# A hybrid transformer block on one core: the masked key products of two scan chunks as one block-diagonal 128 by 128 weight tile

## What is computed

```python
def rwkv_scan(S0, r, w, k, v, a, b, reverse):
    def step(S, inp):
        r_t, w_t, k_t, v_t, a_t, b_t = inp
        sa = jnp.einsum('bhij,bhj->bhi', S, a_t)
        S = S * w_t[:, :, None, :] + sa[..., :, None] * b_t[:, :, None, :] + v_t[..., :, None] * k_t[:, :, None, :]
        return S, jnp.einsum('bhij,bhj->bhi', S, r_t)
    ...
    S, ys = lax.scan(step, S0, xs, reverse=reverse)
```

## Time and profile before

| | |
|---|---|
| median of 3 runs | 2294.09 us (2288.39 to 2295.02) |
| the profiled execution | 2289.43 us, its span 2287.4 us |
| granted TensorE clock, mean over the span | 0.974 |
| PE busy | 2162.4 us, 95% |
| PE weight loads (PEld, beside PE) | 1780.5 us, 78% |
| DVE busy | 958.9 us, 42% |
| POOL busy | 872.0 us, 38% |
| ACT busy | 663.2 us, 29% |

### The profile page before, as it was taken

How to read it: one execution, slowest core, us unless ns; L and a number is a source line. 1 busy time by engine, 2 the same in 40 slices (tenths; PEclk the granted TensorE clock), 3 DMA queues, 4 the chain that set the end, 5 groups by cost and what they waited for, 6 DMA issues and landing times.

```text
span 2287.4 us, 44913 instructions
## 1 busy us (share of the span) xinstructions
PE 2162.4 (95%) x19484; PEld 1780.5 (78%) x19484; DVE 958.9 (42%) x1411; ACT 663.2 (29%) x1178; POOL 872.0 (38%) x602
## 2 busy tenths in 40 slices
PE   6999899989899999999999999989989989999997
PEld 3888477668778888888888778857759867888886
DVE  2002355386743723315142520335476645452452
ACT  3110366632412211102011320146652323221221
POOL 3333333172144224333242542235253144454454
PEclk9999999999997999999999899999999988999999
DMA  7311200210131112222123331120120042333231
GB/s 281 100 52 54 74 2 1 98 38 4 39 130 46 56 56 65 65 65 65 56 74 127 113 112 56 38 74 2 62 74 4 13 158 64 92 101 101 83 111 55
DMA packets 45463, 163.73 MB, mean 72 GB/s; under 512 B 5504, under 2 KB 5504, under 8 KB 45024
## 3 DMA queue, kind: packets, MB, share of 16 engines
q1 hardware_dynamic: 44480, 158.29, 21.2%
q0 software_dynamic: 800, 2.69, 0.4%
HBM read 158.86 MB, written 2.10 MB: 70 GB/s over the span
## 4 chain that ended last, share of the span: by engine, by line
PE 85%; DVE 6%; ACT 4%; issue 3%; POOL 1%; DMA 1%; SPq 0%; DVEq 0%; ACTq 0%; POOLq 0%
PE ps L1567 80%; PE ps L1893 3%; ACT flat L872 1%; DMA flat<-wmod_dram 1%; PE ps L2180 0%; DVE flat L1362 0%; DVE part_h L1436 0%; POOL flat L703 0%; DVE flat L1371 0%; DVE flat L1180 0%; DVE flat L1351 0%; POOL flat L614 0%; ACT hT L886 0%; POOL wparts L568 0%; DVE flat L1416 0%
## 5 line engine op out<-in xcount | busy, mean ns | idle before, releaser
L1567 PE MATMUL ps<-part_hi,wparts 128*128 128x512 f32 (+1 forms) x2640 | 701.9, 352 | 10.1 <-POOL wparts L568 5.9
L1567 PEld LDWEIGHTS ps<-part_hi,wparts 128*128 128x128 f32 x2640 | 468.0, 190 | 82.7 <-DVE part_h L1436 5.5
L1567 PE MATMUL ps<-part_h,wparts 128*128 128x512 f32 (+1 forms) x1320 | 462.9, 351 | 0.0
L1567 PE MATMUL ps<-flat 64*64 64x32 f32 (+8 forms) x8200 | 420.8, 257 | 29.9 <-DVE flat L1371 14.5
L1567 PEld LDWEIGHTS ps<-flat 64*64 64x64 f32 (+4 forms) x8200 | 322.0, 141 | 117.9 <-issue 92.1
L606 POOL TENSOR_TENSOR wparts<-flat,wparts 128x1024 fp32r<-128x1024 f32 x96 | 241.0, 2511 | 411.0 <-ACT wparts L1081 409.6
L1567 PE MATMUL ps<-part_mlp,wparts 128*128 128x512 f32 (+1 forms) x1152 | 309.9, 354 | 0.6 <-issue 0.6
L1567 PEld LDWEIGHTS ps<-part_h,wparts 128*128 128x128 f32 x1320 | 250.9, 190 | 33.8 <-issue 1.7
L1567 PEld LDWEIGHTS ps<-part_mlp,wparts 128*128 128x128 f32 x1152 | 204.9, 189 | 31.3 <-issue 0.7
L1567 PE MATMUL ps<-part_lo,wparts 128*128 128x512 f32 (+1 forms) x576 | 204.0, 354 | 0.0
L1558 DVE TENSOR_TENSOR flat<-flat,ps 128x768 f32<-128x768 f32 (+1 forms) x64 | 52.5, 820 | 355.7 <-PE ps L1567 355.7
(11 more groups left out here) (224 smaller groups left out, 2825.7 us busy)
## 6 DMA issues: line engine op xcount, KB each, us to landing
flat<-w_dram SPq DMA_DIRECT2D x128, 512.0 KB, 3.6
flat<-wmod_dram SPq DMA_DIRECT2D x88, 512.0 KB, 5.9
flat<-win_dram SPq DMA_DIRECT2D x40, 512.0 KB, 3.6
flat<-wout_dram SPq DMA_DIRECT2D x16, 512.0 KB, 3.6
hT<-wmod_dram SPq DMA_DIRECT2D x8, 512.0 KB, 7.7
xT<-xT_dram SPq DMA_DIRECT2D x8, 384.0 KB, 6.4
flat<-rope_dram SPq DMA_DIRECT2D x2, 1024.0 KB, 6.5
out_dram<-xT SPq DMA_DIRECT2D x8, 256.0 KB, 2.1
```

Of the source, the lines that this page charges most:

```text
L1567: return pe.matmul(out, lhsT, rhs, start=start, stop=stop)
```

## The change

The AB part of each half moves out of `ABR` into a new place `DIAG[x][g]`, where each pair of direction and head has a 128 by 128 tile: AB of chunk 0 in the upper left block, AB of chunk 1 in the lower right block, and zeros in the other two. The X group then has 8 matmuls over all 128 rows and columns, each with the same 32 moving columns on 128 partitions. On DVE one mask of 1024 columns becomes three instructions: one for AB of chunk 0 on 64 partitions, one for AB of chunk 1 on the other 64, and one for R on 128 partitions, each of 512 columns. Only the third adds to `s_abm[x]`. ACT writes the tiles with zeros once in a layer, in four copies of 512 columns, before its first evacuation of the recurrence, and DVE waits for that before the first half of step 0. R is packed closer, and its readers follow.

```diff
+        DIAG = ((HALF[0] + 512, F_WORK + W_SCAN + 2 * SCAN_HALF), (RING + 5 * 256, HALF[1] + 512))
...
                 act.wait_ge(s_rp, 12 * l + 12)
                 nc_.activation(gtok[:, 4:6, :], ps[:, 1024:1536].rearrange("p (b f) -> p b f", b=2), ACT.Copy).then_inc(s_rpe, 1)
+                act.wait_ge(s_modps, 5 * l + 4)
+                act.wait_ge(s_side, 7 * l + 4)
+                act.wait_ge(s_prep, 3 * l + 2)
+                for x, g in ((0, 0), (1, 0), (1, 1), (0, 1)):
+                    ins = nc_.activation(cells(-1, DIAG[x][g], [1, 512]), km[:, M_AB:M_AB + 1].to_broadcast([P, 512]), ACT.Copy)
+                ins.then_inc(s_gate, 1)
...
-                        V.tensor_tensor(cells(-1, h + ABR, [256, 4], [1, 256]), bank(-1, o, [256, 4], [1, 256]),
-                                        km[:, M_AB:M_AB + 256].unsqueeze(1).to_broadcast([P, 4, 256]),
+                        if s == 0:
+                            dve.wait_ge(s_gate, 3 * l + 2)
+                        for c in range(2):
+                            V.tensor_tensor(cells(c, DIAG[x][0] + 64 * c, [DIAG[x][1] - DIAG[x][0], 2], [P, 4], C1),
+                                            bank(c, o, [P, 2], [256, 4], C1),
+                                            bass.AP(km, 64 * c * NKM + M_AB, [[NKM, 64], [P, 2], [0, 4], C1]), ALU.mult)
+                        V.tensor_tensor(cells(-1, h + ABR, [P, 4], [64, 2], C1), bank(-1, o + 64, [256, 4], [P, 2], C1),
+                                        bass.AP(km, M_AB + 64, [[NKM, P], [0, 4], [P, 2], C1]),
                                         ALU.mult).then_inc(s_abm[x], 1)
...
                                 for p in range(2):
                                     for f in range(2):
-                                        for c in range(2):
-                                            ins = mm(bank(c, o + g * P + (2 * p + f) * 32, [1, 32]),
-                                                     cells(c, h + ABR + p * 512 + f * 256 + g * P, C1),
-                                                     cells(c, h + TN + g * (256 + half) + (2 * p + f) * 64,
-                                                           [2 * half, 32 // half], [1, half]))
+                                        ins = mm(bank(-1, o + g * P + (2 * p + f) * 32, [1, 32]),
+                                                 cells(-1, DIAG[x][g] + (2 * p + f) * P, [1, P]),
+                                                 cells(-1, h + TN + g * (256 + half) + (2 * p + f) * 64,
+                                                       [2 * half, 32 // half], [1, half]))
                             ins.then_inc(s_X[x], 1)
...
-                                    q, r = h + ABR + p * 512 + f * 256 + g * P + 64, h + TOKS + g * 256 + f * P + p * 64
+                                    q, r = h + ABR + p * 256 + f * P + g * 64, h + TOKS + g * 256 + f * P + p * 64
```

More of the change, by code:

```diff
@@ L1970, in _ @@
                     if n == 2:
-                        pe.wait_ge(s_gate, 2 * l + 1)
+                        pe.wait_ge(s_gate, 3 * l + 1)
                         pe.wait_ge(s_rtab, 64 * (l + 1))
@@ L2098, in _ @@
                                     for f in range(2):
-                                        for c in range(2):
-                                            ins = mm(bank(c, o + g * P + (2 * p + f) * 32, [1, 32]),
-                                                     cells(c, h + ABR + p * 512 + f * 256 + g * P, C1),
-                                                     cells(c, h + TN + g * (256 + half) + (2 * p + f) * 64,
-                                                           [2 * half, 32 // half], [1, half]))
+                                        ins = mm(bank(-1, o + g * P + (2 * p + f) * 32, [1, 32]),
+                                                 cells(-1, DIAG[x][g] + (2 * p + f) * P, [1, P]),
+                                                 cells(-1, h + TN + g * (256 + half) + (2 * p + f) * 64,
+                                                       [2 * half, 32 // half], [1, half]))
                             ins.then_inc(s_X[x], 1)
                         if s == 0 and j == 2:
-                            pe.wait_ge(s_gate, 2 * l + 2)
+                            pe.wait_ge(s_gate, 3 * l + 3)
                             for b in range(NB):
```

## The result

The changed kernel takes 2476.32 us (median of 4 runs, 2467.31 to 2480.82) against 2293.19 us for the kernel before. The ratio is 1.080, with a 95% interval of 1.078 to 1.082: 183 us slower, where 55 us (2349 us) had been forecast and 2370 us was the high end of the range. The profiled execution has a span of 2465.5 us, 178 us more than before.

The account below looks back on a forecast made before the run. PE was taken to set the pace of the levels, with DVE's chain before them in steps 1 and 2. X groups 47.4 plus masks 6.7 and 1.0 made 55 us, so 2349 us (+2.4%), range 2335 to 2370 us.

Parts of the forecast that it names:

- 16 x 0.108 = 1.73 us against 0.94: X groups on PE in the levels: 16 records of 108 ns, +0.79 us a group, +47.4 us over 60 groups.
- The granted clock should stay as it was: Closing expectation for the changed kernel's profile: no change in PE's granted clock, so no time counted for it.
- the price of a narrow record: Sums over tiles, 128 by 128 weights, 1 or 2 columns: 104 to 105 ns, taken as lower bound for a wide record.
- The masks: DVE before the levels: three masks for one, 0.98 us more a half, +6.7 us in steps 1 and 2, +1.0 in step 0.
- The zeros: Four ACT copies a layer, 2.4 us, said to be covered by DVE's work; counted as nothing.
- The floor per instruction: Rival: a PE record costs the same whatever its tile, so the kernel gets faster, about 2282 us; chance 3%.
- the fast full tile: Rival: a full tile loads as fast as one quarter, 59 ns; only the masks' 8 us remain, 2302 us; chance 4%.
- Dearer wide tiles as in the bonus matmuls: Rival: a wide X record costs 120 up to 145 ns, giving 2361 to 2385 us; chance 15%.
- The reading that a quarter of the array loads 64 columns in some 59 ns: From today's record pace on PE: each quarter gives one record every 58.8 ns, and quarters load side by side.

Follow-up runs that it names:

- e10: e5 with the 32 columns of each wide matmul streamed twice: 2350.22 us, ratio 1.026 to the kernel before.
- e5: The kernel before with X groups of 8 matmuls with 128 by 128 identity weights, the masked-key product left out, DVE and ACT unchanged: 2461.18 us, ratio 1.072.
- e11: The kernel before with a 512-column identity matmul before the sums of every second tile after the output projection: 2309.5 us, ratio 1.008.
- e1: The changed kernel with X groups put back to 16 matmuls of 64 by 64 weights; masks, zeros and layout stay: 2339.61 us, ratio 1.021.
- e2: The kernel before with the X group's chunk loop outermost, 8 matmuls in one quarter, then 8 in the other: 2415.78 us, ratio 1.055.
- e6: e1 with four 256-column identity matmuls put where PE waited for the masks of half 1: 2312.43 us, ratio 1.009.
- e8: The kernel before with DVE's first 512-column mask of each half done twice, PE's work unchanged: 2311.52 us, ratio 1.008.

## Why the prediction was wrong

The direction was right and the direct terms were nearly right (55 to 67 us against 55); a whole term was missing, the granted clock.

- **The step that failed** is the one that priced the X group at "16 x 0.108 = 1.73 us against 0.94" for all 60 groups, together with the closing assumption "The granted clock should stay as it was". At full clock a group took 1.78 us in e10 (111 ns per record), and that part is worth some 50 us. The assumption had no row behind it. The wide groups lower the clock by themselves (e5: 379 us at the lower level instead of 119), and then everything on PE in the levels takes 1.8 to 1.9 times as long (1.71 us against 0.94, 3.41 against 1.78), Tp included. That missing term is 111 to 123 us of 178.
- **A row that warned of it was within reach.** I read the price of a narrow record from two runs of 12 in the earlier trace rows, 104 and 105 ns. The same form (one moving column) stands elsewhere in the trace of the kernel before, in one long run. The PE timeline there:

```profile
718.55 16.35 PE L1567 MATMUL ps<-kf,flat 128*128 128x1 f32 x84 [0.26 <-ACT flat L771]
```

And its windows:

```profile
720.00:725.00 5.00, 5.00 (x28) 5.00 (x27) 3.31 (x7) 3.56 (x5) 4.80 (x4) 0.55 0.01 3
725.00:730.00 5.00, 5.00 (x25) 5.00 (x25) 0.00 (x0) 0.00 (x0) 4.92 (x3) 0.50 0.33 105
```

84 records in 16.35 us are 195 ns each. PE is busy for the whole of both windows, and the clock is at 0.5. A long unbroken run of weight loads with next to nothing streamed behind them went with the lower clock in the kernel before, and the change makes the levels more like such runs. The short runs of 12 stood among matmuls of 512 columns at full clock. The row is a warning and not a proof: e11, which put such matmuls into the long run, didn't bring its clock back.
- **The masks.** 0.98 us a half was forecast and 0.87 measured (566.58 to 568.60 us, 2.02 us for three, against 1.15); the direct cost is 6 us in e1, against the 7.7 in the sum. What they set off was missed: the prediction let PE wait and priced the wait at its length. By itself it costs up to 43 us of clock in e1. In the changed kernel it adds little, since the clock is lost anyway; that the two causes overlap is why e1's 48 and e5's 167 don't add up to 183.
- **The zeros** cost nothing seen: DVE's first mask of AB follows L1450 without a wait in both layers.
- **The rivals.** The floor per instruction and the fast full tile are both excluded by 111 to 118 ns per record in e10. Dearer wide tiles as in the bonus matmuls were closest in effect and wrong in cause: 181 ns was the mean of two clock levels, not the price of a tile. The reading that a quarter of the array loads 64 columns in some 59 ns was too high: used alone in e2, a quarter gave a record every 45 ns. No rival dealt with the clock.

The Trainium skill, "TensorE: Matmul & The Clock Gate", section "LDWEIGHTS (loading the stationary operand)", divides the number of columns by 1.2 to get the load in ns; for 128 columns that makes 107 ns, an estimate from its formula. This case's traces agree at full clock within a tenth (111 to 118 ns in e10), and at the lower level the record takes 213 ns. The same page of the Trainium skill, in "HAM oscillation — how this bites in real kernels", ties the fall of the clock to PE being idle while it waits. e1 and e6 agree with that, with an idle time of 1.64 us; e5 against e10 shows a fall with PE never idle in the levels, and there the measurement decides.

Open are which mixture of loads and streamed columns holds the clock, and when a wait sets off a fall: 1.34 us did so once in e8 and once not, and in the kernel before PE waits 1.68 us for POOL at 495.92 us, just ahead of step 0, with the clock at 1.00 in the levels behind it.

## What to carry to other kernels

Fewer and larger matmuls are not less work when their weights change each time. Here two 64 by 64 tiles loaded side by side in different quarters, and a group took 0.94 us; with one 128 by 128 tile in place of each two it took 1.78 us at full clock. Before pricing PE work from a row, look at the granted clock of that row's window and of the longest run of the same form, since the price has two levels and the new pattern may choose the other one. And a wait that is short on PE is priced by the clock behind it too: a busy PE with few columns to stream, or a gap of 1.6 us in front of such work, cost far more here than the time itself.

## What was not expected of the hardware

- A stretch of PE work without any idle time dropped to 1.2 GHz because of what it was made of: wide f32 loads with 32 columns each (clock 0.923), against 0.974 with 64 columns each, for 111 us.
- 64 by 64 tiles, used in one quarter of the array at a time, lost nearly as much clock as full tiles did (0.931 in e2, 0.926 in the changed kernel).
- Behind a wait of 1.64 us in front of the levels the clock was at 0.5 for over 10 us, and filling the wait with unneeded matmuls made the kernel 27 us faster.
- With three masks in place of one, DVE's identity add of 512 columns took up to 2.37 us, where it had taken 0.68 to 1.14. It ran beside POOL's work in those places; what held it was not tested.
